# Moving work earlier in a one-core decoder step: sample attention beside tile 0's dots, ten more weighted rows on TensorE, and w_out pieces over 128 partitions

## What is computed

```
mod = silu(c) @ w_ada + b_ada                      # 6 chunks of 2048
h   = rms_norm(x) * (1 + scale1) + shift1
q, kv (compressed, selected, window), gates, u = split(h @ w_in)
o   = gated sum of three attentions (the samples against a paged cache), and a causal pooling mixer of u
x1  = x + gate1 * (concat(o_nsa, o_pool) @ w_out)
h2  = rms_norm(x1) * (1 + scale2) + shift2
per token: 8 heads, product keys, top 16 of 128 x 128 experts each -> 128 expert ids and logits
y   = x1 + gate2 * sum_k softmax(logit)_k * gelu(h2 . peer_u[id_k]) * peer_v[id_k]
```

## Time and profile before

| what | value |
|---|---|
| median of 3 runs | 2570.46 us (2568.68 to 2578.82) |
| the profiled execution, its own time | 2574.56 us |
| its span | 2572.8 us |
| DVE, POOL, PE busy | 1757.6, 1184.3, 1280.7 us |
| DMA | 944.49 MB, mean 367 GB/s |
| `peer_u` and `peer_v` rows | 640 gathers of 1.05 MB |

### The profile page before, as it was taken

How to read it: one execution, slowest core, us unless ns; L and a number is a source line. 1 busy time by engine, 2 the same in 40 slices (tenths; PEclk the granted TensorE clock), 3 DMA queues, 4 the chain that set the end, 5 groups by cost and what they waited for, 6 DMA issues and landing times.

```text
span 2572.8 us, 17754 instructions
## 1 busy us (share of the span) xinstructions
PE 1280.7 (50%) x6315; PEld 697.2 (27%) x6317; DVE 1757.6 (68%) x2243; ACT 212.5 (8%) x559; POOL 1184.3 (46%) x686
## 2 busy tenths in 40 slices
PE   5699998897490543266884972000015655200000
PEld 2363534482240432143331960000002222000000
DVE  1010112217967977897557667999999998899898
ACT  3110012100001221121001010000000000000000
POOL 1000100002426744575222415678876767788684
PEclk9799898899795655556995985555556677655555
DMA  9949899659999999999998989999999999999897
GB/s 299 332 172 422 324 414 291 208 196 360 388 422 397 377 366 341 405 410 370 344 373 321 414 318 410 366 393 422 422 407 407 400 420 417 417 422 422 366 422 307
DMA packets 163042, 944.49 MB, mean 367 GB/s; under 512 B 34635, under 2 KB 44435, under 8 KB 56830
## 3 DMA queue, kind: packets, MB, share of 16 engines
q0 software_dynamic: 94784, 682.66, 66.0%
q1 hardware_dynamic: 68175, 260.74, 28.2%
HBM read 937.36 MB, written 10.26 MB: 368 GB/s over the span
## 4 chain that ended last, share of the span: by engine, by line
PE 27%; DMA 25%; DVE 20%; POOL 15%; issue 9%; SPq 2%; ACT 1%; POOLq 0%; another core or an unknown queue 0%; DVEq 0%; ACTq 0%
POOL arena L668 11%; DMA arena<-in_peer_u,arena 10%; DMA arena<-in_peer_v,arena 9%; DVE arena L1975 8%; POOL arena L680 4%; DVE arena L1998 4%; DMA arena<-in_w_out 4%; PE PS L1468 3%; PE PS L1445 3%; PE PS L1016 3%; DMA arena<-in_w_ada 3%; PE PS L1166 2%; PE PS L1253 2%; PE PS L966 2%; PE PS L1423 2%
## 5 line engine op out<-in xcount | busy, mean ns | idle before, releaser
L668 POOL DMA_INDIRECT arena<-in_peer_u,arena x256 | 471.7, 1843 | 446.1 <-DVE arena L1975 240.8
L1975 DVE CUSTOM_DVE_ANT_0 arena<-arena 128x2048 f32<-128x2048 f32 x256 | 581.5, 2289 | 118.0 <-DMA arena<-in_peer_u,arena 116.7
L1998 DVE SCALAR_TENSOR_TENSOR arena<-arena 128x2048 f32<-128x2048 f32 x226 | 531.1, 2350 | 136.6 <-DMA arena<-in_peer_v,arena 131.9
L668 POOL DMA_INDIRECT arena<-in_peer_v,arena x256 | 428.3, 1673 | 369.7 <-DVE arena L1998 242.7
L1468 PE MATMUL PS<-arena 128*128 128x512 f32 x240 | 180.3, 921 | 449.9 <-DMA arena<-in_peer_v,arena 449.9
L1468 PEld LDWEIGHTS PS<-arena 128*128 128x128 f32 x240 | 69.5, 304 | 561.4 <-issue 555.1
L1474 PE MATMUL PS<-arena 128*64 128x512 f32 x8 | 5.5, 849 | 346.4 <-DVEq L2041 346.4
L2031 DVE SCALAR_TENSOR_TENSOR arena<-arena 128x2048 f32<-128x2048 f32 x64 | 150.6, 2352 | 10.8 <-DMA arena<-in_peer_v,arena 5.3
L966 PE MATMUL PS<-arena 128*32 128x512 f32 x768 | 119.4, 721 | 69.9 <-DMA arena<-in_w_ada 66.6
L2028 DVE CUSTOM_DVE_ANT_0 arena<-arena 128x2048 f32<-128x2048 f32 x64 | 145.0, 2291 | 8.4 <-DMA arena<-in_peer_u,arena 6.5
L680 POOL DMA_INDIRECT arena<-in_peer_v,arena x64 | 126.4, 1975 | 39.0 <-issue 18.6
(11 more groups left out here) (347 smaller groups left out, 1824.5 us busy)
## 6 DMA issues: line engine op xcount, KB each, us to landing
arena<-in_w_ada SPq DMA_DIRECT2D x96, 1024.0 KB, 12.1
arena<-in_w_in SPq DMA_DIRECT2D x32, 1048.0 KB, 9.2
arena<-in_peer_wq SPq DMA_DIRECT2D x32, 1024.0 KB, 10.2
arena<-in_w_in SPq DMA_DIRECT2D x32, 768.0 KB, 11.2
arena<-in_w_out SPq DMA_DIRECT2D x16, 1024.0 KB, 30.0
arena<-in_w_out SPq DMA_DIRECT2D x32, 512.0 KB, 24.0
arena<-in_peer_u,arena POOLq DMA_INDIRECT x320, 13.9
arena<-in_peer_v,arena POOLq DMA_INDIRECT x320, 15.5
```

What stands on the lines that cost most here:

```text
L668: pool.indirect_dma_start(out=rows_ring[:, k % NROW, :], out_offset=None, in_=tables[kind], in_offset=bass.IndirectOffsetOnAxis(ap=ids[:, ...
L1975: V.tensor_tensor_reduce(out=buf, in0=buf, in1=h2(t), scale=1.0, scalar=0.0, op0=ALU.mult, op1=ALU.add, accum_out=dots[:, t, r:r + 1]).the ...
L1998: V.scalar_tensor_tensor(out=acc[t], in0=rows_ring[:, k % NROW, :], scalar=dots[:, t, r:r + 1], in1=acc[t], op0=ALU.mult, op1=ALU.add).the ...
```

## The change

1. The start: pages two at a time after each w_ada piece, w_cmp and its matmuls later in the lists of SP and TensorE by the order below.
2. Head pieces of w_out: one DMA over 128 partitions for each 8 KB piece, and for `out1` one for each of the two row blocks.
3. Beside the rows: `Q_PAUSE` 12 to 0, `K_PAUSE` 20 to 2, fewer rows per unit (3), sample attention and the first `add1` beside dots 0; the second `add1` and both halves of tile 1's expert choice beside sums 0; the first half of tile 2's choice beside dots 1. ACT's exponentials are put where they no longer stand ahead of copies of w_in's products.
4. Ten rows of sums 0 go to TensorE, added in dots 1.
5. The window cache and pooling state copies are issued by POOL when the first half of `compress_sample` is done.

```diff
-Q_PAUSE, K_PAUSE, S_PAUSE, OUT_PAUSE, WQ_PAUSE = 12, 20, 3, 20, 30
+Q_PAUSE, K_PAUSE, S_PAUSE, OUT_PAUSE, WQ_PAUSE = 0, 2, 3, 16, 34
...
             elif kind == "out":
-                for gi in range(2):
-                    eng.dma_start(dst[64 * gi:64 * gi + 64, 0:D], w_out_nsa[n // 4, gi, :, n % 4, :]).then_inc(done, 16)
+                eng.dma_start(dst[:, 0:D], w_out_nsa[n // 4, :, :, n % 4, :]).then_inc(done, 16)
...
                 if c < 4:
-                    for gi in range(2):
-                        eng.dma_start(pair[64 * gi:64 * gi + 64], w_out_nsa[c // 2, gi, :, 2 * (c % 2):2 * (c % 2) + 2, cols]).then_inc(done, 16)
+                    for i in range(2):
+                        eng.dma_start(pair[:, i, :], w_out_nsa[c // 2, :, :, 2 * (c % 2) + i, cols]).then_inc(done, 16)
...
-        PE_ROWS = [BASE[3] + n for n in range(3, 120, 4)]
+        PE_ROWS = [BASE[1] + n for n in range(83, 120, 4)] + [BASE[3] + n for n in range(3, 120, 4)]
...
-            cmp_pages(0)
-            load(6, 10)
+            cmp_pages(0, 4)
+            for i in range(6):
+                load(6 + i, 7 + i)
+                cmp_pages(4 + 2 * i, 6 + 2 * i)
             cmp_weights(0)
-            cmp_pages(4)
-            load(10, 14)
-            cmp_pages(8)
-            load(14, 18)
-            cmp_pages(12)
+            load(12, 16)
             cmp_weights(1)
-            load(18, n_start)
+            load(16, n_start)
...
+            pool.wait_ge(s_cmp, 1)
+            pool.dma_start(O["win_sample"][:, 0:PAST - DT].rearrange("b s c g d -> b (s c g d)"),
...
-            expert_exp(0)
+            expert_exp(0, 0)
...
             A(qkr[:, 1:3, NH:24], qkr[:, 1:3, NH:24], sqrt).then_inc(s_zrt, 1)
+            expert_exp(0, 1)
...
-            def beside_sums():
-
                 yield from pause(S_PAUSE)
                 dve.wait_ge(s_bs, 32)
...
-                for h in range(2):
-                    yield from pause(OUT_PAUSE)
-                    yield from add1(h)
+                yield from pause(OUT_PAUSE)
+                yield from add1(0)
+
+            def beside_sums():
+
                 yield
+                yield from add1(1)
                 rms2(1)
...
                 yield from pause(WQ_PAUSE)
                 yield from experts(1, 0)
+                yield from paced(experts(1, 1), 2)
 
             def beside_dots1():
-                yield from paced(experts(1, 1), 2)
-                yield from pause(2)
+                dve.wait_ge(s_prow, by_pe(BASE[2]))
+                link(V.tensor_tensor(acc[0], acc[0], PS[:, 0:4, :].rearrange("p a b -> p (a b)"), ALU.add))
+                dve.sem_inc(s_facc, 1)
+                yield
+                yield from paced(experts(2, 0), 3)
                 shares(1)
```

More of the change, by code:

```diff
@@ L397, in build @@
             k = slot_number(i)
-            count[k % 12] += 32 if p[0] == "out" and p[1] < 8 or p[0] == "out1" and p[2] < 4 else 16
+            count[k % 12] += 32 if p[0] == "out1" and p[2] < 4 else 16
             arrived.append(count[k % 12])
@@ L487, in cmp_weights, with cmp_pages @@
                         sp.dma_start(WC[c][64 * gi:64 * gi + 64, gp], wc[c, gi, gp]).then_inc(s_wc[c], 16)
-            def cmp_pages(m0):
-                for m in range(m0, m0 + 4):
+            def cmp_pages(m0, m1):
+                for m in range(m0, m1):
                     wait(sp, s_ct, m - 3)
@@ L808, in _, with expert_exp @@
                 A(sc0[:, 0, 4 * k:4 * k + 4, :].rearrange("p a b -> p (a b)"), PS[:, 4 + k, :], copy).then_inc(s_sc, 1)
[L810 to L814 removed]
+            def expert_exp(t, half):
+                w = gw[:, t, half * HH:(half + 1) * HH]
+                act.wait_ge(s_e2, 2 * t + half + 1)
+                A(w, w, exp).then_inc(s_e2x, 1)
             def gelu(t):
@@ L1037, in _ @@
             pages(0, 4)
-            ada(0, 6, 10)
-            pages(4, 8)
-            ada(0, 10, 14)
-            pages(8, 12)
-            ada(0, 14, 16)
-            ada(1, 0, 2)
-            pages(12, 16)
-            ada(1, 2, 4)
+            for i in range(6):
+                ada(0, 6 + i, 7 + i)
+                pages(4 + 2 * i, 6 + 2 * i)
             pe.wait_ge(s_ctc, 16)
@@ L1412, in _ @@
                     for m in range(2):
-                        last = spread(4 + 2 * k + m, 2, 2 * h + m, selT[:, k, :])
+                        last = spread(4 - 4 * h + 2 * k + m, 2, 2 * h + m, selT[:, k, :])
                 last.then_inc(s_gp, 1)
-                if h == 1:
-                    pe.wait_ge(s_gb, 12)
+            pe.wait_ge(s_gb, 12)
+            for h in range(2):
                 for cc in range(NK // 2):
@@ L1455, in _, with pe_rows @@
             ada(5, 0, NK)
+            def pe_rows(t):
+                mine = [(j, k) for j, k in enumerate(PE_ROWS) if BASE[2 * t + 1] <= k < BASE[2 * t + 2]]
+                for j, k in mine:
+                    pe.wait_ge(s_diag, j + 1)
+                    pe.wait_ge(s_row[k % NROW], 16 * (k // NROW + 1))
+                    for n in range(4):
+                        last = mm(PS[:, n, :], diag[:, j % 2, :], rows_ring[:, k % NROW, n * SECTION:(n + 1) * SECTION],
+                                  start=(j == mine[0][0]), stop=(j == mine[-1][0]))
+                    last.then_inc(s_prow, 1)
+            pe_rows(0)
             pe.wait_ge(s_adaC, 6)
@@ L1459, in _ @@
             for i in range(8):
-                spread(i, 5, i % 4, selT[:, i // 4, :]).then_inc(s_g2p, 1)
-            pe.wait_ge(s_g2, 8)
-            for j, k in enumerate(PE_ROWS):
-                pe.wait_ge(s_diag, j + 1)
-                pe.wait_ge(s_row[k % NROW], 16 * (k // NROW + 1))
-                for n in range(4):
-                    last = mm(PS[:, n, :], diag[:, j % 2, :], rows_ring[:, k % NROW, n * SECTION:(n + 1) * SECTION],
-                              start=(j == 0), stop=(j == len(PE_ROWS) - 1))
-                last.then_inc(s_prow, 1)
-            pe.wait_ge(s_facc, 2)
+                wait(pe, s_g2, i - 3)
+                spread(4 + i % 4, 5, i % 4, selT[:, i // 4, :]).then_inc(s_g2p, 1)
+            pe.wait_ge(s_facc, 1)
+            pe_rows(1)
+            pe.wait_ge(s_facc, 3)
             for n in range(4):
@@ L1947, in beside_sums1 @@
                 yield
-                for half in range(2):
-                    yield from paced(experts(2, half), 2)
+                yield from paced(experts(2, 1), 2)
                 yield from pause(2)
```

58 lines of the change are left out of this document (24 added, 34 removed).

## The result

The change makes the kernel slower: 2868.59 us (median of 4 runs, 2866.24 to 2870.48) against 2569.57 us (4 runs), ratio 1.1164, 95% interval 1.1148 to 1.118. That is 299 us.

The account below looks back on a forecast made before the run. From dots 0 on the DMA engines were taken as the bound, VectorE close behind; before, tile 0's chain. 2574.6 - 6 + 82 - 25 + 38 + 123 - 7 = 2779.6, less 4.1 for the median: 2776 us, range 2565 to 2870.

Parts of the forecast that it names:

- the chain's term: Tiles 1 and 2 beside dots 0: removed pauses let the 961.5 us run nearer capacity, -25 us (0 to -56).
- Two engines for a head piece: New w_out loads: source's outermost size 2 gives 2 of 16 engines, 53 GB/s, 19.9 us a piece.
- full width: Rival, chance 0.18: 128-partition loads get 16 engines; 2502 us, with 42 us of w_out's gain coming back as waits.
- Tile 0, +82: w_out for tile 0: loads on 2 engines end at 568 us, matmuls at 570 against 487, +82 us.
- bound of +110: w_out for tile 0: upper bound, if the query's weights behind in SP's queue come late as well.
- The value page, +38: Samples' value page behind the first two head pieces of out1 in SP's queue: rows wait, +38 us (0 to +40).
- `out1`, +123: w_out for tiles 1 and 2, two halves beside rows: +43 and +80, together +123 us (-42 to +150).
- Start -6: Start: first compress_sample work hidden beside loads, two copies take some back; -6 us (-20 to +10).
- dots 1 -7: Dots 1: half an expert choice goes, half of tile 2's comes; 335.5 to 329 us, -7 (-10 to +5).
- four tighter steps: Dots 0: q, k, pooling and scores wait for just-made products, 5 to 10 us each; about 30 of 56 come back.
- bound of -98: Dots 0 and sums 0: best case, 354 MB without the copies at 410 GB/s take 863 us, not 961.5.
- Ten rows, 0: Ten sums on TensorE: VectorE's 24 us lie beside rows coming every 2.49 us anyway, so 0 us gained.

Follow-up runs that it names:

- e8: Kernel before with only the window cache's copy given as 16 parts, the part outermost (16 in place of 8): 2562.67 us, ratio 0.9976.
- e10: Kernel after with head pieces over 128 partitions read from other (wrong) rows of w_out, 8 runs of 16, the 8 outermost: 2632.4 us, ratio 1.0247.
- e4: Kernel after with only the head pieces of out1 loaded by two DMAs of 64 partitions; tile 0's stay over 128: 2697.9 us, ratio 1.0507.
- e3: Kernel after with only tile 0's head pieces loaded by two DMAs of 64 partitions; out1 stays as in after: 2750.8 us, ratio 1.0715.
- e1: Kernel after with both sets of w_out's head pieces loaded by two DMAs of 64 partitions, as before the change: 2586.09 us, ratio 1.0068.
- e6: Kernel after with head-piece loads of 64 partitions, 5 rows per sample unit in place of 3, both add1 in sums 0: 2558.72 us, ratio 0.9953.
- e7: Kernel after with head-piece loads of 64 partitions and without the ten rows of sums 0 on TensorE and their addition in dots 1: 2594.78 us.
- e9: Kernel after with head pieces over 128 partitions read from other (wrong) rows of w_out, 16 runs of 8, the 16 outermost: 2580.58 us, ratio 1.0042.
- e5: Kernel after with each head piece loaded by four DMAs of 32 partitions that alternate between partitions 0 to 63 and 64 to 127: 2582.39 us.
- e2: Kernel before with only w_out's head pieces changed to loads over 128 partitions, two for a piece of out1: 2863.77 us, ratio 1.1146.

## Why the prediction was right, and where it was off

The direction, the place and the mechanism were right. That 2868.59 still lies within a range up to 2870 is luck: tile 0 was above its upper bound, and the rest of the change cost 17 us where every bound of the chain's term was a gain or nothing.

*Two engines for a head piece.* Right, to the number: 53 GB/s at a share of 0.13, on the queue for which the trace of before had no row. It rested on the copy's row at outermost 8, and e8 and e10 show that the reason was right. The reading of the row was less so: "beside nothing else" is true of neither half of that window, in which rows moved as well. It came out at 8 engines because the rows that were left had to use the copy's 8. The rival "full width" named the copy's other queue as its hope; that was no reason.

*Tile 0, +82.* Measured 113 in the trace, 112 and 118 by e4 and e3, just past the bound of +110. The mechanism was right and the term was mis-sized. The loads end at 593.6 in place of 568. Of these 26 us, 14 lie ahead of the first head piece, which came at 425 and not at 411 (389 + 2.5 + 19.9): until some 405 us all 16 engines were busy, and had w_ada's last pieces to move as well (421 GB/s from 390 to 400 us). The other 12 lie in the seven pairs after it, 168.6 us in place of 7 x 22.4 = 157. Part of that is at the end, where the query's weights share the engines and all 16 are busy at 276 GB/s (560 to 570 us), and not at the 422 by which the other pieces had been counted. Then the last matmuls took 6.7 us and not 2. Late weights of the query, for which the upper bound had been kept, did not come (TensorE's 512 matmuls with them take 57.6 us, before 57.3).

*The value page, +38, and `out1`, +123: 161.* Measured by e3 and e1: 165. The parts, as waits in after less those in e1: 34 us at the page, 66 at the first `add1` (+43 had been counted), some 79 at the second (+80). Together that is 179, more than the 165 to 171 by which the times differ, so some is made up elsewhere. The page's own wait in after is 59 us and above its bound of +40, but 25 of it stand in e1 with the old loads: they belong to the new order, and in the prediction's sum nothing stood for them.

*Start -6, chain -25, dots 1 -7: -38.* Measured +17 by e1, the only term of the wrong sign, and 55 of the missing 93 us. Dots 1 was right (-5.5 in the windows), the start gave 1 us. The step that failed is the sentence that four tighter steps at 5 to 10 us bring back about 30 of 56: the eight sample units and the first `add1` were not among the four. A unit has a chain of 13.57 us through TensorE and ScalarE, and with 3 rows in place of 6 it is no longer covered, which makes five waits of 4.2 us; with them come the 25 us for the value page and 18 us at the first `add1`. The row of before that would have shown the first is the unit's distance, 16.9 us with 6 rows, which the prediction did not read. e6 shows that these places are worth 27 us; what each is worth alone stays open. The bound of -98 was also too wide by some 10 us: the two copies were put at 8.6 MB, read and written, but the 377 and 410 GB/s count each byte once, and in that measure their packets are 4.3 MB.

*Ten rows, 0.* Measured -9 by e7. DMA's share of 0.97, a mean over dots 0 and sums 0, was taken for each part of sums 0; where expert choices stand beside the rows, VectorE is the bound (e7's window).

*The full-width rival, 2502 us.* Its price was wrong as well: e9 has that width, and takes 2581 us. As far as e9's rows of w_out stand for the right ones, the change with 16 engines would not have been faster but some 10 us slower than before. Its 42 us for w_out came from reading 282 GB/s as the cost of 64 partitions, which e5 and e9 don't bear out. Nor does it decide from 8 engines on: the 7.13 us of the earlier trace rows are 16 matmuls, those of two pieces, and one piece's take 3.6 to 3.7. In e10, with 8 engines, TensorE waits and tile 0 ends 16 us late.

The terms by the runs: 112 (`out`), 165 (`out1` and page), 6 (both together) and 17 (the rest). That they make 299 to within a microsecond is no check, since the last two are what is left over; e2, where the other three make 295 in the old order, shows that the terms shift by some 12 us with the order around them.

## What to carry to other kernels

Look at the outermost size of both sides of a DMA before its partitions: a merge of two loads into one that reads well in the code leaves 2 of 16 engines if it puts a 2 outermost, an eighth of the rate, and everything behind it in the queue pays. A transfer that moves at a share well below 1 is the sign of it, but look at what else moves in the window, and for how long, before you divide. Cutting such a copy into 16 parts changes one line on each side. And when pauses are removed, compare the latency of one unit of the chain with the rows that are left in it, unit by unit: in these runs rows in between cost nothing while the DMA engines stayed busy (e6), and a wait cost what the ring of 6 rows couldn't hold (e1).
